# A ring of expert rows with six slots in place of eight, and ten in place of six query blocks kept on chip between token tiles

## What is computed

```python
q = (xf @ w_q).reshape(N, PEER_HEADS, 2, PEER_QHALF)           # 8 heads, 2 x 128
s = jnp.einsum('nhpd,hpkd->nhpk', q, subkeys)                  # 128 keys each
top_s, top_i = lax.top_k(s, PEER_TOPK)                         # 16 of each half
cand_s = top_s[:, :, 0, :, None] + top_s[:, :, 1, None, :]     # 256 pairs
best_s, best_pos = lax.top_k(cand_s, PEER_TOPK)                # 16 experts a head
idx, g = ..., jax.nn.softmax(best_s, axis=-1)
act = jax.nn.gelu(jnp.einsum('nd,nhkd->nhk', xt, u_tab[it]))
y = jnp.einsum('nhk,nhkd->nd', gt * act, v_tab[it])
```

## Time and profile before

| | |
|---|---|
| median of 3 runs | 2533.29 us (2528.17 to 2534.04) |
| profiled execution | 2530.09 us, span 2528.3 us |
| TensorE busy | 2247.8 us (89%) |
| VectorE busy | 1659.6 us (66%) |
| ScalarE, GpSimd busy | 911.9 us (36%), 871.4 us (34%) |
| moved by DMA | 945.41 MB, 374 GB/s over the span |

### The profile page before, as it was taken

One profiled execution on the slowest core, in us unless ns is written; L12 is line 12 of the kernel. 1 busy time (PEld: TensorE's weight loads), 2 busy tenths in 40 slices (PEclk: granted clock), 3 DMA queues, 4 the chain that ended last, 5 costly groups with the idle time before them and its releaser, 6 DMA issues.

```text
span 2528.3 us, 29579 instructions
## 1 busy us (share of the span) xinstructions
PE 2247.8 (89%) x9630; PEld 1265.8 (50%) x9630; DVE 1659.6 (66%) x3972; ACT 911.9 (36%) x2668; POOL 871.4 (34%) x796
## 2 busy tenths in 40 slices
PE   9998889998988989899999898989899989977776
PEld 7887644554444535544535554435555536522222
DVE  3864366666665677566776566767567766776664
ACT  2232133333343433243443334533244533423232
POOL 0012033334343343343443343334343344344442
PEclk9999999999999999999999999999999999999999
DMA  5420489999999999999999999999999999999996
GB/s 194 133 85 19 185 314 421 421 421 421 422 418 421 415 386 421 421 420 422 419 395 421 421 421 420 422 417 407 421 416 391 410 421 420 414 416 421 421 417 287
DMA packets 152443, 945.41 MB, mean 374 GB/s; under 512 B 16955, under 2 KB 19147, under 8 KB 53861
## 3 DMA queue, kind: packets, MB, share of 16 engines
q0 software_dynamic: 110592, 805.36, 77.0%
q1 hardware_dynamic: 41700, 138.20, 14.2%
HBM read 942.44 MB, written 1.05 MB: 373 GB/s over the span
## 4 chain that ended last, share of the span: by engine, by line
PE 45%; DMA 39%; DVE 7%; ACT 4%; issue 3%; POOL 1%; DVEq 0%; SPq 0%; ACTq 0%; POOLq 0%
DMA arena<-in_uv,idx 39%; PE bank L1875 26%; PE bank L354 7%; DVE arena L1903 4%; PE bank L1532 2%; PE bank L1520 2%; ACT arena L1941 1%; PE bank L825 1%; PE bank L585 1%; PE bank L841 1%; PE bank L1427 1%; ACT arena L1929 1%; PE bank L812 1%; PE bank L866 1%; ACT arena L1935 1%
## 5 line engine op out<-in xcount | busy, mean ns | idle before, releaser
L1875 PE MATMUL bank<-arena 128*128 128x512 f32 x3072 | 1449.6, 617 | 246.5 <-ACT arena L1941 240.7
L1960 POOL DMA_INDIRECT arena<-in_uv,idx x768 | 843.7, 1099 | 1435.6 <-PE bank L1875 1298.8
L1875 PEld LDWEIGHTS bank<-arena 128*128 128x128 f32 x3072 | 574.0, 195 | 968.8 <-issue 614.3
L1903 DVE CUSTOM_DVE_ANT_0 arena<-arena,h 128x1024 f32<-128x1024 f32 x512 | 627.3, 1225 | 415.7 <-DMA arena<-in_uv,idx 400.9
L1929 ACT ACTIVATE arena<-arena 128x2 f32<-128x2 f32 x384 | 78.2, 204 | 1226.7 <-DVE arena L1903 1226.5
L1903 DVE CUSTOM_DVE_ANT_0 arena<-arena 128x1024 f32<-128x1024 f32 x256 | 313.7, 1225 | 218.0 <-DMA arena<-in_uv,idx 210.7
L354 PEld LDWEIGHTS bank<-xT,weights 128*128 128x128 f32 x2032 | 279.8, 191 | 57.5 <-issue 39.6
L354 PE MATMUL bank<-xT,weights 128*128 128x128 f32 (+2 forms) x2032 | 299.6, 303 | 0.0
L1941 ACT ACTIVATE arena<-const,arena 128x128 f32<-128x128 f32 x768 | 260.5, 386 | 0.0
L1935 ACT ACTIVATE arena<-arena 128x1 f32<-128x1 f32 x768 | 184.8, 288 | 12.6
L1929 ACT ACT_TABLE_LOAD x73 | 93.7, 1283 | 1.3
(11 more groups left out here) (331 smaller groups left out, 1766.4 us busy)
## 6 DMA issues: line engine op xcount, KB each, us to landing
weights<-in_w_q SPq DMA_DIRECT2D x50, 512.0 KB
weights<-in_w_in SPq DMA_DIRECT2D x38, 512.0 KB
weights<-in_a_fm SPq DMA_DIRECT2D x28, 512.0 KB
arena<-in_uv,idx POOLq DMA_INDIRECT x768
weights<-in_a_out SPq DMA_DIRECT2D x16, 512.0 KB
weights<-in_b_fm SPq DMA_DIRECT2D x16, 512.0 KB
weights<-in_b_out SPq DMA_DIRECT2D x16, 512.0 KB
arena<-in_w_q SPq DMA_DIRECT2D x14, 512.0 KB, 13.1
```

Of the source, the lines that this page charges most:

```text
L1875: ins = nc.tensor.matmul(acc[:, :], diag[:, e % DIAGS, :], ring[:, e % RING, at:at + 512], start=first, stop=last)
L1903: V.tensor_tensor_reduce(out=u, in0=u, in1=x, scale=1.0, scalar=0.0, op0=ALU.mult, op1=ALU.add, accum_out=dots[:, unit % 2, kx:kx + 1]).th ...
L1960: nc.gpsimd.indirect_dma_start(out=ring[:, s, :], out_offset=None, in_=io[f"uv{unit // PH // NT}"], in_offset=bass.IndirectOffsetOnAxis(ap ...
```

## The change

RING goes from 8 to 6. The arena room of the two slots (4 x 1024 numbers a partition) becomes `kept`, four more homes for query blocks, and CACHED goes from 6 to 10: blocks 6 to 9 of layers 1 and 2 are now loaded once a layer and not once a tile. Their loads are issued behind four further entries of the plan: `a_out` 6, 7, 0, 1 in layer 1, `b_v` 6, 7 and `b_out` 6, 7 in layer 2.

```diff
-CACHED = 6
+CACHED = 10
...
-RING = 8
+RING = 6
...
         ring = G.take(RING, 2 * D)
+        kept = G.take(4, D)
...
-            return xn[:, 0, :] if n == 1 else G.view(mem_at, D)
+            if j == 5:
+                return xn[:, 0, :] if n == 1 else G.view(mem_at, D)
+            return kept[:, j - 6, :]
...
-                else:
+                elif j == 5:
                     sp.wait_ge(sem("dots"), TILE_EXPERTS)
+                else:
+                    sp.wait_ge(sem("w_o_last"), 2)
...
-            for n, name in ((1, "a_r"), (2, "b_v")):
+            behind = {1: [("a_r", 0, j) for j in range(6)] + [("a_out", 0, kc) for kc in OUT_ORDER],
+                      2: [("b_v", 0, kc) for kc in range(KC)] + [("b_out", 0, kc) for kc in OUT_ORDER]}
+            for n in (1, 2):
                 for j in range(CACHED):
-                    load_blocks(sp, at, first[name, 0, j] + 1)
-                    at = first[name, 0, j] + 1
+                    load_blocks(sp, at, first[behind[n][j]] + 1)
+                    at = first[behind[n][j]] + 1
                     load_cached(sp, n, j)
```

More of the change, by code:

```diff
@@ L1622, in load_cached @@
                     sp.wait_ge(sem("squares_1"), 1)
+                elif j == 5:
+                    sp.wait_ge(sem("dots"), TILE_EXPERTS)
                 else:
-                    sp.wait_ge(sem("dots"), TILE_EXPERTS)
+                    sp.wait_ge(sem("w_o_last"), 2)
             else:
```

## The result

| | changed kernel | kernel before, on the same chip |
|---|---|---|
| median | 2580.47 us (2571.55 to 2584.97, 4 runs) | 2532.44 us (2528.17 to 2534.04, 4 runs) |
| ratio | 1.0186 [1.0171, 1.0200] | |
| profiled execution | 2571.55 us, span 2569.7 us | 2530.09 us, span 2528.3 us |

The change makes the kernel 1.9% slower. The forecast was 2551, its range ended at 2568: the sign is right, the size is too small by a factor of 2.6 (48 us in place of 18.5).

The account below looks back on a forecast made before the run. DMA bytes, plus every moment in which the engines run dry, were taken as the bound. Gain -8.5, start +5.0 and stalls +22.0 summed to +18.5 us, giving 2551 us; overall range 2529 to 2568.

Parts of the forecast that it names:

- the sign: Whole kernel: slower, forecast 0.7%; slower by over 0.3% was given a chance of 0.68.
- the start: Before expert 0 is used: two gathers move behind the gap of the DMA engines, costing 5.0 us.
- The gain: Second tile's query steps, layers 1 and 2: eight loads of 512 KB less save 5.0 + 3.5 = 8.5 us.
- The loads moved to an earlier stretch: First tile: kept blocks' loads only move to an earlier stretch running at the same rate, counted at nothing.
- the stalls, 22.0: Where VectorE's long mixer operations delay dots: six named stalls plus 3.3 for shallower dips cost 22.0 us.
- steady stretches cost nothing: Undisturbed expert stream: slot turn 6.9 plus gather latency 6.0 make 12.9 us, under six gathers' 14.9, so no loss.
- The shallow dips: Some five slices between 407 and 417 GB/s: 3.3 us together, between 0 and 10.
- F: Latency of a gather with nothing queued ahead: taken as 6.0 us, between at least about 4.5 and 7.9.
- Rival 3: Steady stream: gather latency 7.9 makes the turn 14.8 against 14.9, six slots break the pace; +36.5, 2570 us; chance 0.08.
- Rival 1: All gathers: latency only 4.4 to 4.5 us, stalls shrink to 9.7; +6, 2539 to 2541 us, no change; chance 0.18.
- Rival 2: Stalls: SP's queued weight loads fill the DMA holes, so stalls cost nothing; faster, 2524 to 2526 us; chance 0.13.
- Rival 4: Query steps: TensorE paces them, gain 0 to 3 instead of 8.5; 2557 to 2560 us; within the forecast's 0.61.

Follow-up runs that it names:

- ring6: Kernel before with RING alone cut from eight slots to six, six query blocks kept as before: 2586.31 us, 1.0197.
- ring7: Kernel before with RING alone cut from eight slots to seven: 2540.66 us, 1.0027.
- thin8: Kernel before, eight slots, loading only 64 of 1024 columns of query blocks 6 to 9 in the second tiles: 2526.03 us, 0.9967.
- early6: Changed kernel with layer 1's four new kept query blocks loaded at some 330 us, in the start's idle stretch: 2581.69 us, 1.0189 against the kernel before.
- half6: Kernel before with six slots and VectorE's dots over 512 of 1024 numbers: 2558.79 us, 1.0110.
- nogate6: Kernel before with six slots and ScalarE's multiplication with the softmax weights left out: 2575.32 us, 1.0165.
- all three edits: Kernel before with six slots, the mixers' long operations cut short, dots over half the numbers, no multiplication with softmax weights: 2540.81 us, 1.0030.
- exp6: Kernel before with six slots and the softmax's exponential made with the already loaded gelu function: 2597.36 us, 1.0253.
- ring5: Kernel before with RING alone cut from eight slots to five: 2833.08 us, 1.1172.
- both6: Kernel before with six slots, dots over half the numbers and no multiplication with the softmax weights: 2554.94 us, 1.0071.
- nogate8: Kernel before, eight slots, with ScalarE's multiplication with the softmax weights left out: 2532.51 us, 0.9988.
- mixhalf6: Kernel before with six slots, the mixers' long operations cut short and dots over half the numbers: 2545.51 us, 1.0051.

## Why the prediction was right and wrong

**Right.** The bound, the places of the stalls and the sign. At the start dot 16 is 5.2 us late (forecast 5.0). Part of the closeness is luck, since traces differ by some us ahead of the stream; counted from dot 0 it is 5.3 here, 4.8 in ring6 and 2.6 in ring7, as two gathers and one should give (5.0 and 2.5). The gain was forecast at 8.5 and is 8.4 in thin8, with an interval of 4.6 to each side; the changed kernel's second query steps give 4.2 and 3.8 where 5.0 and 3.5 were said. The loads moved to an earlier stretch were counted at nothing: they show as a step of 4.1 us where they went (experts 176 to 192), and as 3.5 given back in the first tile's query steps (222 to 254). The bytes, gather 6's issue at 347.99, the pair's pace of 4.97 and the new dip near 2100 came as said. The gather in the chain was said to be 9.4 us and is 8.5 to 9.1.

**Wrong: the stalls, 22.0.** The lags over the six stalls that the prediction names (experts 192 to 208, 320 to 336, 464 to 480, 560 to 576, 592 to 608 and 640 to 656) are 6.7, 7.5, 4.1, 5.2, 3.3 and 2.4 us, 29.2 in all, against 4.2, 3.0, 1.5, 4.5, 3.5 and 2.0, 18.7 in all. The last three were nearly right, the first three are 2.5 to 4.5 us too small. Two things were mis-sized. The wait from issue to use was taken at 6.0, and is 6.9 at the first stall, 0.84 of it a longer issue on GpSimd. And each stall was priced by the first gather that comes late, after which the ring was to run at 2.49 us an expert again. It doesn't: the turn in the mixer's stretch is 9.9 us and not the 6.3 of the late stream, so that the ring goes on at 2.80 there. Both are read at the first stall; the second and third were not taken apart in the same way. One reading was wrong as well: 7.9 us is not the shortest wait in the kernel before. Gather 208 itself, issued at 917.39, is used at 924.77, after 7.4.

**Wrong above all: "steady stretches cost nothing".** The shallow dips were given 3.3 us, "nearer to 0 because eight slots hardly dip there". The last dot is 41.5 us late; less 5.2 for the start and 29.2 for the named stalls, and plus the 8.4 gained, that leaves 15 for everything else, nearly five times the term. The step that failed is 6.9 + 6.0 = 12.9 under 14.9. F was meant as the latency of a gather with nothing ahead, and as that 6.0 is not too small: the quickest gathers of the traces take 5.3 to 6. But in the steady stream a gather has others beside it. TensorE returns the slots in pairs (late in the stream GpSimd's issues come by turns 1.7 and 3.3 us apart), and gathers share the DMA engines: 8.2 us is the median with five slots. So the sum was about 15, not 12.9. Rival 3 had this case, with its condition ("F at 7.9", "14.8 against 14.9"), its witness (dots wait a little for data nearly everywhere) and its price, 2570 and more. It was given 0.08. "Turns of 12.3 to 12.9 us leave 2 us" was the reason, and that reason used the F in question. A late gather in the steady stretch looks like this in the changed kernel:

```profile
2464.95 1.80 POOL L1965 DMA_INDIRECT arena<-in_uv,idx  x1 [2.82 <-PE bank L1880]
...
2473.88 1.23 DVE L1908 CUSTOM_DVE_ANT_0 arena<-arena,h 128x1024 f32<-128x1024 f32 x1 [2.86 <-DMA arena<-in_uv,idx]
```

and for the same expert, 736, in the kernel before, where the same long issue does not hold the pace: the gather leaves 12.2 us ahead of its dot and not 8.9.

```profile
2421.25 1.92 POOL L1960 DMA_INDIRECT arena<-in_uv,idx  x1 [2.82 <-PE bank L1875]
...
2433.45 1.22 DVE L1903 CUSTOM_DVE_ANT_0 arena<-arena,h 128x1024 f32<-128x1024 f32 x1 [1.15 <-DMA arena<-in_uv,idx]
```

**The other rivals.** Rival 1 (a gather of 4.4 to 4.5 us) falls with the shortest gather of all traces, 5.3, and its 2539 to 2541 with the time. Rival 2 (weights fill the holes) falls with the holes of 190 and 232 GB/s; early6 did fill the one of the start, and gained nothing. Rival 4 (the kept loads don't leave the path) falls with thin8.

**What stays open.** Whether the pairing of the slots' return or the sharing of the DMA engines makes most of the 8.2 us was not separated. That half6 gains 20 us and nogate6 5 fits VectorE's freed time, the larger cut of its turn and GpSimd's shorter issues, and these three were not tried apart. The lower clock of TensorE in the stalls (0.50 in the first) was not taken out either. And the 11 us that are left with all three edits have no name.

## What to carry to other kernels

The depth that a ring of prefetched tiles needs is its turn plus the latency of a fetch **in company**, over the pace. Near that number the loss sets in steeply: 7, 53 and 299 us for one, two and three slots fewer. Take the latency from a trace of the same pattern, and the turn from the stretch where the engines are fullest; if a value chosen within a range decides whether there is any slack, the case without slack deserves more than the 0.08 that it got here. A cheap test before buffers are given up: lower the slot count alone, to the number planned, and look for slices that fall off the ceiling in the undisturbed part. One slot fewer would not have warned here, since ring7 still has 420 GB/s from 2300 to 2500 us; ring6 has 407.

## What the hardware showed beside that

GpSimd's issue of a gather takes 0.94 us in the median and up to 1.99, for the same instruction:

```profile
L1965 POOL DMA_INDIRECT arena<-in_uv,idx x724: 932/937/1987, 401.2 to 2498.2; - x181
```

What makes them long can be read off by laying the issues beside VectorE's dots. In the changed kernel 185 issues begin while a dot still has more than 0.25 us to run, and nearly all of them end 0.81 us after that dot's end, however long it had to go. Of the 486 that begin with no dot running or about to start, the median is 0.94 us, and three take over 1.2. The kernel before and ring6 show the same (195 and 210 such issues, 0.81 us). Gather 202 above is one: the dot of 919.42 ends at 920.64, and the issue that began at 919.67 ends at 921.45. So a dot on VectorE holds GpSimd's issue, and half as long a dot holds it less: the mean issue is 0.98 us in half6 and 1.11 in ring6. How much of the loss with six slots comes by this way was not tried.

The granted clock of TensorE differs between the traced executions ahead of the stream, where their code is the same. In exp6 it is 0.64 from 10 to 20 us and 0.92 from 20 to 40, so that a good part of this stretch runs at the lower of its two levels, 1.2 GHz, and the engine does 42 matmuls in the first of these rows:

```profile
0.00:10.00 10.00, 7.29 (x12) 2.94 (x12) 2.68 (x16) 4.62 (x10) 0.20 (x4) 1.00 0.79 273
10.00:20.00 10.00, 9.69 (x42) 8.32 (x42) 0.63 (x4) 3.18 (x8) 0.00 (x0) 0.64 0.64 261
20.00:40.00 20.00, 20.00 (x85) 16.59 (x85) 0.89 (x2) 3.06 (x5) 0.00 (x0) 0.92 0.30 105
```

In ring6 it stays at 2.4 GHz, with 59:

```profile
10.00:20.00 10.00, 10.00 (x59) 8.43 (x59) 0.34 (x3) 5.18 (x9) 0.00 (x0) 1.00 0.61 249
```

In both the engine was busy for 7 to 8 of the 10 us before. ring5, both6 and nogate8 show it as exp6 does (0.59, 0.60 and 0.62 in the same row), and in all four the first gather is issued at 329.1 to 329.6 us; in the other traces that is between 321.5 and 328.5 (mixhalf6, whose clock is 1.00 in that row), so the clock is not all of it. What tips it was not tried, and with one trace of each kernel it can't be said whether it goes with the kernel or with the execution. It is worth knowing when kernels are compared whose difference is under 0.3%: part of it can be made in the first 40 us.
